# One inference step of a mixture-of-experts backbone on one core: down projection interleaved into the next expert's hidden tiles, expert loops written out, activation tables loaded once per stretch

## What is computed

```python
def rmsnorm(x, g):
    return x * rsqrt(mean(x * x, -1) + EPS) * g

def expert_choice_ffn(x, w_router, w_gate, w_up, w_down):
    aff = softmax(x @ w_router)
    gsel, idx = top_k(swapaxes(aff, 1, 2), cap)
    xs = x[bidx, idx]
    hdn = silu(xs @ w_gate) * (xs @ w_up)
    out = (hdn @ w_down) * gsel[..., None]
    return zeros_like(x).at[bidx, idx].add(out)
```

## Time and profile before

| what | value |
|---|---|
| runs timed | 3190.57, 3200.09, 3201.3 us (median 3200.09) |
| profiled execution | 3194.56 us, its span 3192.6 us |
| PE busy | 2937.7 us (92% of the span) |
| DVE busy | 963.5 us (30%) |
| ACT busy | 567.1 us (18%) |
| DMA | 545.49 MB, mean 171 GB/s |
| granted TensorE clock | 0.949 of full speed |

### The profile page before, as it was taken

One profiled execution on the slowest core, in us unless ns is written; L12 is line 12 of the kernel. 1 busy time (PEld: TensorE's weight loads), 2 busy tenths in 40 slices (PEclk: granted clock), 3 DMA queues, 4 the chain that ended last, 5 costly groups with the idle time before them and its releaser, 6 DMA issues.

```text
span 3192.6 us, 43116 instructions
## 1 busy us (share of the span) xinstructions
PE 2937.7 (92%) x18357; PEld 2213.0 (69%) x18357; DVE 963.5 (30%) x2409; ACT 567.1 (18%) x1279; POOL 95.9 (3%) x145
## 2 busy tenths in 40 slices
PE   4999999788999999994999989999896999999994
PEld 1565489556778877771665479999845778887773
DVE  1100156542011100002577346677544011100002
ACT  2100111340000000002474112222251000000002
POOL 0000000000000000000000000000000000000000
PEclk8999998888999999997899989999997999999997
DMA  8312000247999999949211000000026899998892
GB/s 355 115 53 73 0 1 1 66 157 255 309 308 305 308 310 305 308 158 385 71 53 53 14 1 1 1 1 1 7 80 239 302 307 307 313 309 303 305 309 82
DMA packets 257932, 545.49 MB, mean 171 GB/s; under 512 B 15233, under 2 KB 23817, under 8 KB 251657
## 3 DMA queue, kind: packets, MB, share of 16 engines
q1 hardware_dynamic: 156617, 328.64, 29.1%
q10 hardware_dynamic: 93600, 188.75, 16.9%
q0 software_dynamic: 7584, 26.22, 3.3%
HBM read 517.89 MB, written 25.70 MB: 170 GB/s over the span
## 4 chain that ended last, share of the span: by engine, by line
PE 85%; DVE 6%; DMA 5%; ACT 3%; issue 1%; SPq 1%; DVEq 0%; POOL 0%; ACTq 0%
PE ps L1210 29%; PE ps L1221 14%; PE ps L809 9%; PE ps L819 6%; PE ps L1145 4%; DMA slots<-in_w_ada_dram 3%; PE ps L1107 3%; PE ps L810 2%; PE ps L1089 2%; PE ps L886 2%; PE ps L1121 1%; PE ps L766 1%; PE ps L797 1%; PE ps L956 1%; PE ps L972 1%; PE ps L968 1%
## 5 line engine op out<-in xcount | busy, mean ns | idle before, releaser
L1210 PEld LDWEIGHTS ps<-wk,slots 128*128 128x128 f32 x6144 | 691.1, 192 | 16.5 <-issue 16.0
L1210 PE MATMUL ps<-wk,slots 128*128 128x80 f32 x6144 | 689.9, 275 | 0.0
L1221 PE MATMUL ps<-qkv,og 128*80 128x512 f32 x1024 | 446.7, 594 | 2.4 <-DVE og L1757 1.3
L1221 PEld LDWEIGHTS ps<-qkv,og 128*80 128x80 f32 x1024 | 151.0, 150 | 275.4 <-issue 268.0
L809 PE MATMUL ps<-hT,slots 128*128 128x512 f32 x640 | 333.3, 603 | 3.3 <-ACT hT L457 3.3
L1210 PE MATMUL ps<-wk,qkv 128*128 128x80 f32 x2048 | 233.9, 275 | 0.0
L810 PEld LDWEIGHTS ps<-hT,slots 128*128 128x128 f32 x640 | 123.2, 193 | 156.1 <-issue 156.1
L1210 PEld LDWEIGHTS ps<-wk,qkv 128*128 128x128 f32 x2048 | 231.3, 192 | 0.0
L819 PE MATMUL ps<-slots,hT 128*128 128x512 f32 x480 | 208.9, 595 | 0.0
L1733 DVE COPY idc<-idT 80x1 uint32 (+1 forms) x32 | 4.8, 149 | 615.1 <-DMA moe_d<-og,idc 615.0
L819 PEld LDWEIGHTS ps<-slots,hT 128*128 128x128 f32 x480 | 91.6, 191 | 111.6 <-issue 111.3
(11 more groups left out here) (262 smaller groups left out, 3134.8 us busy)
## 6 DMA issues: line engine op xcount, KB each, us to landing
slots<-in_w_gate_dram ACTq DMA_DIRECT2D x60, 2048.0 KB, 10.1
qkv<-in_w_down_dram SPq DMA_DIRECT2D x34, 2048.0 KB, 9.8
slots<-in_w_up_dram SPq DMA_DIRECT2D x32, 2048.0 KB, 10.1
qkv<-in_w_up_dram SPq DMA_DIRECT2D x32, 2048.0 KB, 7.9
qkv<-in_w_down_dram ACTq DMA_DIRECT2D x30, 2048.0 KB, 7.8
slots<-in_w_ada_dram SPq DMA_DIRECT2D x24, 2048.0 KB, 12.8
slots<-in_w_in_dram SPq DMA_DIRECT2D x16, 2048.0 KB, 8.3
slots<-in_w_out_dram SPq DMA_DIRECT2D x4, 2048.0 KB, 16.4
```

The costliest lines, as they stand in the source:

```text
L1210: ins = mm(PS[:, j, fb * CAP:(fb + 1) * CAP], slot[j][:, kt, fb * P:(fb + 1) * P], xsT[q][:, kt, :], start=(kt == 0), stop=(kt == KT - 1))
L1221: ins = mm(PS[0:CAP, 4 + j, :], hdT[:, ft, :], slot[4 + j][:, ft, :], start=(ft == 0), stop=(ft == KT - 1))
```

## The change

1. **PE.** `up(e, j)` is a block of 32 gate or up matmuls as before. For e of 1 and more, blocks 2 and 3 of expert e are run as `up_and_down(e, j)`: 32 times one piece of expert e-1's down matmul, 128 output columns wide instead of 512, and one gate or up matmul. `turn(e+1)` stands between blocks 1 and 2. Down of expert 15 runs alone at the end, 512 wide. `hdT` has two buffers, the second in `wk`. `moe_used` is split into `gu_used` (4 per expert) and `dn_used` (2).
2. **Loads.** SP issues all pieces, in the order 0, 1, 2 of e+1, 4 of e, 3 of e+1, 5 of e; ACT issues none.
3. **POOL and DVE.** The index tile `idT` is used directly (no `pick`), gathers run up to four experts ahead on two semaphores.
4. **Loops.** All expert loops are written out on all engines.
5. **ACT.** `log_and_exp()` loads the table set that has both Ln and Exp at the start, ahead of each `mixer_tail`, of layer 1's first norm and of the last norm. The Ln and Exp of `inverse_root` in these stretches then have no load of their own; those inside layer 1's conv loop, between Tanh, keep theirs.

```diff
+                for j in range(6):
+                    expert_load(0, j)
+                for e in range(EX):
+                    for j in (0, 1, 2, 4, 3, 5):
+                        if j < 4 and e + 1 < EX:
+                            sp.wait_ge(S("gu_used"), L * PER["gu_used"] + 4 * e + j + 1)
+                            expert_load(e + 1, j)
+                        elif j >= 4 and e:
+                            sp.wait_ge(S("dn_used"), L * PER["dn_used"] + 2 * (e - 1) + j - 3)
+                            expert_load(e, j)
...
+                for e in range(4):
+                    gather(e)
+                for e in range(EX):
+                    if e + 4 < EX:
+                        gather(e + 4)
+                    scatter(e)
...
+            def log_and_exp():
+                nc.scalar.preload_act_table_set("natural_log_exp_and_others")
...
             def mixer_tail(L):
 
                 i = 2 * L + 1
+                log_and_exp()
                 gate_tile(L, 0)
...
+                def up_tile(e, j, i):
+
+                    fb, kt = divmod(i, KT)
+                    return mm(PS[:, j, fb * CAP:(fb + 1) * CAP], slot[j][:, kt, fb * P:(fb + 1) * P],
+                              xsT[e % 2][:, kt, :], start=(kt == 0), stop=(kt == KT - 1))
+
+                def down_tile(e, j, i):
+
+                    c, ft = divmod(i, KT)
+                    return mm(PS[0:CAP, 4 + j, c * P:(c + 1) * P], hdT[e % 2][:, ft, :], slot[4 + j][:, ft, c * P:(c + 1) * P],
+                              start=(ft == 0), stop=(ft == KT - 1))
...
+                def up_and_down(e, j):
+
+                    up_ready(e, 2 + j)
+                    if j == 0:
+                        pe.wait_ge(S("hidden"), L * PER["hidden"] + 2 * e)
+                    down_ready(e - 1, j)
+                    for i in range(32):
+                        dn = down_tile(e - 1, j, i)
+                        ins = up_tile(e, 2 + j, i)
+                    dn.then_inc(S("dn_used"), 1)
+                    ins.then_inc(S("gu_used"), 1)
...
+                for e in range(EX):
+                    pe.wait_ge(S("xs_in"), L * PER["xs_in"] + e + 1)
+                    up(e, 0)
+                    up(e, 1)
+                    if e + 1 < EX:
+                        turn(e + 1)
+                    for j in range(2):
+                        if e:
+                            up_and_down(e, j)
+                        else:
+                            up(e, 2 + j)
+                down(EX - 1)
```

More of the change, by code:

```diff
@@ L330, in _, with expert_load @@
                     sp.dma_start(xn_d[t * P:(t + 1) * P, :], o[:, t, :]).then_inc(S("xn_out"), 16)
[L331 to L336, removed]
+                def expert_load(e, j):
+                    sp.dma_start(slot[j], w_expert(L, e, j)).then_inc(land[j], 16)
                 sp.wait_ge(*unit_used(L, MIX - 1))
                 sp.wait_ge(S("x_new"), L * PER["x_new"] + 10)
[L340 to L342 removed]
+                for j in range(6):
[8 more added lines that the diff above has]
+                            expert_load(e, j)
                 sp.wait_ge(S("scattered"), L * PER["scattered"] + 16 * EX)
@@ L700, in experts, with gate_half @@
[L700 to L706, removed]
+                def gate_half(e, hf):
+                    act.wait_ge(S("gu_used"), L * PER["gu_used"] + 4 * e + 2 * hf + 1)
+                    if e:
+                        act.wait_ge(S("hidden"), L * PER["hidden"] + 2 * (e - 1) + hf + 1)
+                    A(eb[hf], PS[:, 2 * hf, 0:320], ACT.Tanh, scale=0.5).then_inc(S("gexp"), 1)
@@ new lines, in out_half @@
+                def out_half(e, hf):
+                    act.wait_ge(S("dn_used"), L * PER["dn_used"] + 2 * e + hf + 1)
+                    if hf == 0 and e >= 2:
+                        act.wait_ge(S("scattered"), L * PER["scattered"] + (e - 1) * 16)
+                    A(osb[e % 2][0:CAP, hf * HC:(hf + 1) * HC], PS[0:CAP, 4 + hf, :], ACT.Copy,
+                      scale=gsel[0:CAP, e:e + 1]).then_inc(S("o_ready"), 1)
+                for e in range(EX + 1):
+                    for hf in range(2):
+                        if e < EX:
+                            gate_half(e, hf)
+                    for hf in range(2):
+                        if e:
+                            out_half(e - 1, hf)
@@ L1200, in turn @@
                     ins.then_inc(S("xs_turned"), 1)
[L1202 to L1209, removed]
-                                ins = mm(PS[:, j, fb * CAP:(fb + 1) * CAP], slot[j][:, kt, fb * P:(fb + 1) * P],
-                                         xsT[q][:, kt, :], start=(kt == 0), stop=(kt == KT - 1))
-                        ins.then_inc(S("moe_used"), 1)
@@ L1214, in down @@
-                def down(e, q, first):
-                    pe.wait_ge(S("hidden"), L * PER["hidden"] + e * 2 + 2)
+                def up_tile(e, j, i):
[6 more added lines that the diff above has]
+                              start=(ft == 0), stop=(ft == KT - 1))
@@ new lines, in up_and_down, with down @@
+                def up_and_down(e, j):
[3 more added lines that the diff above has]
+                    down_ready(e - 1, j)
+                    for i in range(32):
+                        dn = down_tile(e - 1, j, i)
+                        ins = up_tile(e, 2 + j, i)
+                    dn.then_inc(S("dn_used"), 1)
+                    ins.then_inc(S("gu_used"), 1)
+                def down(e):
+                    pe.wait_ge(S("hidden"), L * PER["hidden"] + 2 * e + 2)
@@ L1779, in experts @@
+                tokens(0)
+                for e in range(EX):
+                    hidden(e, 0)
+                    if e + 1 < EX:
+                        tokens(e + 1)
+                    hidden(e, 1)
                 dve.wait_ge(S("g2b"), L * PER["g2b"] + 4)
```

164 lines of the change are left out of this document (56 added, 108 removed).

## The result

The changed kernel takes **3117.05 us** (median of 4 runs, 3109.07 to 3120.4) beside 3200.12 us of the kernel before on the same chip. The ratio is 0.9743 with the interval 0.9716 to 0.977: faster by 2.6%, 83 us. The forecast was 3098 with a range of 3070 to 3145: the sign and the range held, and the time is 19 us longer than the point. The profiled execution is one of the four, 3118.63 us with a span of 3116.7. Two later comparisons of the same pair, on other occasions, gave 0.9733 and 0.9742.

What follows compares the result with a forecast made beforehand. The prediction took the experts as PE-bound, with DMA close behind. Two expert stages gain 71.2 us and table loads 25, together 96 off the profiled 3194.56, giving 3098 us, range 3070 to 3145.

Steps and rivals of the forecast that it cites:

- The pair: Expert blocks on PE: two down and two up passes, alternating, cost 0.403 us instead of 0.438; a middle expert 40.7 instead of 43.1.
- Rival 1: Alternating expert blocks: the load after each switch between weight kinds is not hidden; 3442 us, or 3309 for one switch; chance 0.05.
- rival 3: Expert stages: DMA sets the period, an expert stays at 43.1 us and only the tables gain; 3170 us, halfway 3135; chance 0.07.
- Rival 4: Alternating expert blocks: passes interleave singly, down, up, down, up, so a pair costs 0.363 us; 3021 us in all; chance 0.03.
- Rival 2: Expert passes: no load hides under a stream using the same array rows; pair 0.721 us, 3709 us in all; chance 0.02.
- The tables: ACT's table loads, 1.28 us each, leave the chain in both mixer tails and the last norm: 25 us, bounds 10 to 35.
- The wait for piece 5: End of each expert stage: expert 15's last 2 MB piece needs 7.9 us to land, so PE waits about 1 us.
- The other terms of the stage: Per layer: expert 0 without down 29.0 us, 15 experts 610 less 0.6, last down 13.96, bare wait for hidden values 0.75.
- Code and queue: Expert stages: written-out loops and all loads on SP's queue cost nothing; an expert's weights take 32.4 us, under 40.7.

## Why the prediction was right, and where its sizes were off

**The pair: right.** The step "a pass costs the longer of its own stream and the next pass's load" gave 0.403 us for a pair and 40.7 for an expert; the trace has 0.40 and 40.72. Undoing the alternation alone brought back 43.04 and all of the experts' gain, and two other widths came out within 1% of the same rule. The rule holds for the sum and not for each pass: by the starts in the trace, the two down and two up passes take 0.112, 0.109, 0.072 and 0.112 us, where the prediction had 0.110, 0.1115, 0.1115 and 0.070, so the up passes come the other way round. Rival 1 (the switch shows) would have put the period over 47 with pieces of 128 columns, rival 3 (DMA) would have shown PE waiting for pieces in mid-stage; neither is there. Rival 4 (single passes by turns) falls by the rows at 827.13, which come in twos.

Rival 2 was also a rule of the Trainium skill (TensorE: Matmul & The Clock Gate, Part 3, The mechanism): a load overlaps a running matmul only where the row groups differ. All five periods disagree with it; by that rule the pair would have taken 0.72 us, and the trace has 0.40. So that sentence of the section does not hold for these passes; why the loads can overlap is not shown.

**The tables: right in kind, mis-sized.** The step that failed is "from 657.92 on six loads, two for each of three tiles, stand in the chain that ends in out(4) at 672.37, so 7.7 us". The chain does pass through these loads, as it follows ACT and DVE back from out(4). But PE was at work on out(3) beside it until 669.32, and its transposes until 671.2, so the chain had only 1.14 us of advantage over PE's own queue. Taking away 7.7 us of loads makes PE's queue the later of the two, and 1.1 us is all it returns. The term for two tails was 15.4, and the gap in each was 1.1. The other parts held: 2.6 behind each out(4), 1.3 at the start of layer 1's tail, 3.1 in the last norm (measured 2.6 to 2.8, 1.3, 3.0). The prediction's lower bound, 10 "if DVE or PE's order eats half of the tails", comes nearest to the 12.3 us of the rows. By the times of whole runs the tables are worth 12 to 21, so part of that size stays open.

**The wait for piece 5: right in kind, mis-sized.** "A 2 MB piece needs 7.9 us to land" took the median of other transfers, and holds for a piece with nothing beside it, as the run with the last piece early shows. This one took 9.86 and 10.04 us, with expert 14's scatter of 0.33 MB beside it, which the prediction left out; that scatter follows from the same event, the end of expert 14's down. From the first down block to the second it is 8.76 and 9.30 us instead of 6.94 without a wait, so 1.8 and 2.4 us were lost for a forecast of 1, and in layer 1 another 1.7 at the lower clock behind the wait. The other terms of the stage were 1 us short: with the piece loaded early it takes 654.0 to 654.4 with no wait for it at all.

**Sum.** 71.2 + 25 = 96 us were forecast against the profiled execution. The profiled span of the changed kernel is 76 us shorter: 65 in the two stages (6 less than forecast) and 12.3 from the tables (13 less), with 1.5 us of drift in the mixers the other way. The medians differ by 83.

**Code and queue: right.** The written-out loops raise the instruction fetches from 99 to 168 packets, and no wait of PE ends on one. SP alone carries all weights at 321 GB/s (325 were forecast), a share of 0.92, and in mid-stage PE waits for none.

## What to carry to other kernels

Where two kinds of matmul share PE, one bound by its stream and one by its weight load, alternate them so that each load runs under the other's stream, and choose the width of the piece so that its stream just covers the next load (128 columns was the best of the four widths here, counting the 512 of the kernel before): wider pieces cover fewer loads, narrower ones add loads of their own. A stall that the chain shows in front of an engine is worth only its lead over that engine's own queue, so read the engine's timeline beside the chain before pricing it. And after a pipeline is tightened look at its last step, where a buffer comes free late and a transfer has nothing left to hide behind.

## What had not been expected of the hardware

One scatter of 0.33 MB cost a transfer of 2 MB, otherwise alone, 2 us: 9.9 to 10.0 us to land in the changed kernel, 7.9 without the scatter when the last piece is loaded early. A wait of 2.2 us on PE in layer 1 was followed by a block at a granted clock of 0.80 (8.79 us for 7.09), while a wait of 1.67 us in layer 0 and one of 1.85 us in another run of the same kernel were not. With pieces of 64 columns the four down passes between two up matmuls took 0.27 us in the chain where the rule gave 0.32, and the two up passes 0.24 where it gave 0.18, so that the group came out at 0.51 instead of 0.503: the rule held for the sum of a group better than for its passes.
